# LayerNorm 1's weight and offset folded into the MoE modulation, its seeds moved to VectorE, and three pieces of work cut in halves

## What is computed

```python
u = x * (1 + sc1) + sh1                                    # modulation from the condition c
mix = concat(mLSTM heads(u), gated convolution(u)) @ w_out
x = layer_norm(ALPHA * x + (1 + gt1) * mix, ln1_g, ln1_b)  # LayerNorm 1
u = x * (1 + sc2) + sh2                                    # MoE modulation
y = hier_moe(u, ...)                                       # best of 4 groups, then 2 of its 4 experts
x = layer_norm(ALPHA * x + (1 + gt2) * y, ln2_g, ln2_b)    # LayerNorm 2
```

## Time and profile before

| | us |
|---|---|
| median of 3 runs | 835.89 (835.6 to 835.93) |
| profiled execution | 835.82 |
| its span in the trace | 834.1 |
| outside the span | 1.7 |
| PE busy | 795.4 (95% of the span) |
| DVE busy | 418.3 (50%) |
| HBM to chip, mean over the span | 359 GB/s |

### The profile page before, as it was taken

How to read it: one execution, slowest core, us unless ns; L and a number is a source line. 1 busy time by engine, 2 the same in 40 slices (tenths; PEclk the granted TensorE clock), 3 DMA queues, 4 the chain that set the end, 5 groups by cost and what they waited for, 6 DMA issues and landing times.

```text
span 834.1 us, 9198 instructions
## 1 busy us (share of the span) xinstructions
PE 795.4 (95%) x3779; PEld 419.0 (50%) x3801; DVE 418.3 (50%) x869; ACT 101.3 (12%) x237; POOL 29.1 (3%) x72
## 2 busy tenths in 40 slices
PE   8999999999999999999979999989899999999994
PEld 3575588445344434444347658844444434443431
DVE  0189888974423332332265985676533332333135
ACT  2111000023011001101111100002311101110110
POOL 3000000620000000000010000000000000000000
PEclk9999999999999999999999999999999999999998
DMA  9998998997999999999999699366699999999991
GB/s 317 389 387 315 388 388 328 362 380 297 390 412 414 415 411 413 415 411 412 411 388 337 224 359 386 140 248 255 226 383 411 414 415 409 415 416 409 414 391 57
DMA packets 90654, 299.29 MB, mean 359 GB/s; under 512 B 4153, under 2 KB 4441, under 8 KB 82417
## 3 DMA queue, kind: packets, MB, share of 16 engines
q1 hardware_dynamic: 86960, 291.60, 90.2%
q0 software_dynamic: 2592, 7.04, 2.2%
q10 hardware_dynamic: 1056, 0.03, 0.1%
HBM read 297.60 MB, written 1.05 MB: 358 GB/s over the span
## 4 chain that ended last, share of the span: by engine, by line
PE 85%; DMA 6%; DVE 4%; issue 3%; ACT 1%; POOL 1%; POOLq 0%; DVEq 0%; ACTq 0%
PE bank L647 22%; PE bank L603 17%; PE bank L671 12%; PE bank L634 8%; PE bank L620 7%; PE bank L828 7%; DMA ring<-in_w_up_dram 6%; PE bank L693 4%; PE bank L504 2%; PE bank L514 1%; PE bank L581 1%; PE bank L655 1%; PE bank L701 1%; ACT uT L923 1%; PE bank L531 0%
## 5 line engine op out<-in xcount | busy, mean ns | idle before, releaser
L603 PE MATMUL bank<-uT,ring 128*128 128x256 f32 x640 | 140.4, 380 | 0.0
L603 PEld LDWEIGHTS bank<-uT,ring 128*128 128x128 f32 x640 | 121.0, 190 | 19.6 <-issue 3.6
L647 PE MATMUL bank<-ring,qT 128*64 128x512 f32 x448 | 99.4, 594 | 2.8 <-issue 2.8
L671 PE MATMUL bank<-ring,hb 128*64 128x512 f32 x448 | 99.6, 595 | 1.4 <-ACT hb L949 1.4
L647 PE MATMUL bank<-ring,uT 128*64 128x512 f32 x448 | 99.2, 593 | 1.1 <-DMA ring<-in_w_up_dram 1.1
L1073 DVE SCALAR_TENSOR_TENSOR bench<-ring,cond,bench 128x512 f32<-128x512 f32 x126 | 94.7, 752 | 4.5
L1248 DVE SCALAR_TENSOR_TENSOR kT<-bank,share,gate_row 128x512 f32<-128x512 f32 x32 | 24.0, 749 | 90.0 <-PE bank L671 90.0
L634 PEld LDWEIGHTS bank<-ccT,X 128*128 128x128 f32 x512 | 61.5, 197 | 13.2 <-issue 11.4
L634 PE MATMUL bank<-ccT,X 128*128 128x128 f32 x512 | 64.6, 285 | 0.2
L647 PEld LDWEIGHTS bank<-ring,uT 128*64 128x64 f32 x448 | 31.6, 137 | 63.9 <-issue 60.2
L647 PEld LDWEIGHTS bank<-ring,qT 128*64 128x64 f32 x448 | 32.2, 137 | 61.7 <-issue 60.8
(11 more groups left out here) (252 smaller groups left out, 646.4 us busy)
## 6 DMA issues: line engine op xcount, KB each, us to landing
ring<-in_w_gate_dram SPq DMA_DIRECT2D x28, 2048.0 KB, 17.6
ring<-in_w_up_dram SPq DMA_DIRECT2D x28, 2048.0 KB, 17.8
ring<-in_w_down_dram SPq DMA_DIRECT2D x28, 2048.0 KB, 16.0
ring<-in_w_ada_dram SPq DMA_DIRECT2D x24, 2048.0 KB, 18.4
ring<-in_w_in_dram SPq DMA_DIRECT2D x14, 2048.0 KB, 17.7
ring<-in_w_out_dram SPq DMA_DIRECT2D x4, 2048.0 KB, 14.9
bench<-in_w_gate_dram SPq DMA_DIRECT2D x4, 2048.0 KB, 10.1
bench<-in_w_up_dram SPq DMA_DIRECT2D x4, 2048.0 KB, 17.8
```

The source lines that it names most:

```text
L603: last = pe.matmul(bank[4 + (b0 + q) % 4][:, 0:SEQ], w[:, kc, q * P:(q + 1) * P], uT[:, kc, :], start=(kc == 0), stop=(kc == KC - 1))
L647: last = pe.matmul(bank[bk][CAP * j:CAP * (j + 1), :], xg[b][:, 4 * h + k, CAP * j:CAP * (j + 1)], ring[s[h]][:, 4 * j + k, :], start=(h = ...
L671: last = pe.matmul(bank[6 + half][CAP * j:CAP * (j + 1), :], hhT[:, f, CAP * j:CAP * (j + 1)], ring[s[h]][:, 4 * j + 2 * i + half, :], sta ...
```

## The change

1. LayerNorm 1 leaves X without weight and offset: one `tensor_scalar` (subtract mean, times root) takes the place of `centre` and `finish`. `moe_shift_scale` takes weight and offset into scale and shift: scale' = scale * g, shift' = shift + scale * b. For that `b_ada_col` also holds columns of `ln1_g` and `ln1_b`, loaded at the start.
2. The seeds are ALPHA * (X * g + b). DVE writes them in pair 0, in eight instructions (`seed`); ACT's four copies go. POOL loads the rows of LayerNorm 2 only after `seeded`, because `seed` still reads those of LayerNorm 1.
3. The last block of the output projection (second token half, last 512 columns) is cut into two of 256 columns, the second in bank 7, and `add` follows piece by piece. `bn_stats` works on 256 columns everywhere.
4. X of the second token half is finished in column halves (`half_ready`, then `x_ready`), in both norms. The transposes follow half by half; for the MoE they run in the order `by_half` (chunks 0, 1, 4, 5, then 2, 3, 6, 7). One `stay_busy` matmul goes at the start of layer 1. The last output DMA becomes two.
5. `gate_up` waits for ACT's half of the gathered tokens before its first weight tile and for DVE's half before its second.
6. Of the small loads at the start, six become five, and these are bigger.

```diff
+        def out_pieces(t, half):
+            if t == 0 or half == 0:
+                return [(bank[2 * t + half][:, :], slice(0, COLS))]
+            return [(bank[3][:, 0:SEQ], slice(0, SEQ)), (bank[7][:, 0:SEQ], slice(SEQ, COLS))]
+
+        by_half = [c for half in range(2) for c in range(KC) if c // 2 % 2 == half]
+        in_halves = [(slice(0, COLS), half_ready), (slice(COLS, D), x_ready)]
...
+            sp.dma_start(b_moe_rows[4:6, :, :], ln1_g.rearrange("l (r n) -> r l n", n=COLS)).then_inc(cols_landed, 16)
+            sp.dma_start(b_moe_rows[6:8, :, :], ln1_b.rearrange("l (r n) -> r l n", n=COLS)).then_inc(cols_landed, 16)
...
+            for cols, done in in_halves:
+                sp.wait_ge(done, 2 * DEPTH if done is half_ready else 2 * T * DEPTH)
+                sp.dma_start(out[0, P:SEQ, cols], X[:, 1, cols]).then_inc(stored, 16)
...
                 load_gate_row(l, 1)
+                pool.wait_ge(seeded, l + 1)
                 load_norm_rows(l, 1)
...
-                pe.wait_ge(main.xg_act, n + 1)
-                pe.wait_ge(main.xg_dve, n + 1)
-                gate_up(4, b, s[0:2], lambda i: expert_arrived(pe, l, i, p), main.gate)
+                def here(i):
+                    pe.wait_ge((main.xg_act, main.xg_dve)[i], n + 1)
+                    expert_arrived(pe, l, i, p)
+
+                gate_up(4, b, s[0:2], here, main.gate)
...
-                    for t in range(T):
-                        transpose_half(t, x_ready, 2 * T * l - T + t + 1, straight)
-                        if t == 0:
-                            stay_busy(5, 5)
+                    transpose_half(0, [(x_ready, 2 * T * l - T + 1)] * 2, straight, range(KC))
+                    stay_busy(4, 5)
+                    transpose_half(1, [(half_ready, 2 * l), (x_ready, 2 * T * l)], straight, range(KC))
...
-                act.wait_ge(cleared, l + 1)
-                act.wait_ge(x_ready, 2 * T * l + T)
-                for b in range(4):
-                    last = act.activation(bank[b][:, :], X[:, b // 2, b % 2 * COLS:(b % 2 + 1) * COLS], ACT.Copy, scale=ALPHA)
-                last.then_inc(seeded, 1)
...
+                link(dve.tensor_tensor(view(scale2[:, :]), of[:, :, 2:4, :], view(scale), ALU.add))
+                dve.tensor_tensor(mod[:, 3, :], scale2[:, :], weight, ALU.mult)
+                dve.tensor_tensor(view(mod[:, 2, :]), of[:, :, 0:2, :], view(shift), ALU.add)
+                link(dve.tensor_tensor(offset2[:, :], scale2[:, :], offset, ALU.mult))
+                dve.tensor_tensor(mod[:, 2, :], mod[:, 2, :], offset2[:, :], ALU.add).then_inc(mod_moe_ready, 1)
...
                 def finish(t):
                     newton(t, 1, rs_ready, 2 * T * l + t + 1)
-                    dve.scalar_tensor_tensor(out=X[:, t, :], in0=X[:, t, :], scalar=rstd[:, t:t + 1],
-                                             in1=ln_b[:, :], op0=ALU.mult, op1=ALU.add).then_inc(x_ready, 1)
+                    for cols, done in ([(slice(0, D), x_ready)], in_halves)[t]:
+                        dve.tensor_scalar(X[:, t, cols], X[:, t, cols], mv[:, t, 0:1], rstd[:, t:t + 1],
+                                          ALU.subtract, ALU.mult).then_inc(done, 1)
...
+            def seed(l):
+                dve.wait_ge(rows_landed, 16 * (4 * l + 2))
+                dve.wait_ge(cleared, l + 1)
+                for b in range(4):
+                    cols = slice(b % 2 * COLS, (b % 2 + 1) * COLS)
+                    link(dve.scalar_tensor_tensor(out=tmp[:, :], in0=X[:, b // 2, cols], scalar=ALPHA, in1=ln_g[:, cols],
+                                                  op0=ALU.mult, op1=ALU.mult))
+                    last = dve.scalar_tensor_tensor(out=bank[b][:, :], in0=ln_b[:, cols], scalar=ALPHA, in1=tmp[:, :],
+                                                    op0=ALU.mult, op1=ALU.add)
...
                 for p in range(PAIRS):
                     n, b = PAIRS * l + p, p % 2
+                    if p == 0:
+                        seed(l)
                     if p + 1 < PAIRS:
                         xg_half(main, n + 1, 1 - b)
```

More of the change, by code:

```diff
@@ L328, in released @@
             elif kind == "wout":
[L329 removed]
+                eng.wait_ge(mix_done, 5 * l + (2, 5)[i])
             elif i >= 4:
@@ L575, in wait_block, with transpose_half @@
                         pe.wait_ge(proj_dve, 8 * l + b - 19)
-            def transpose_half(t, ready, value, cols):
-                pe.wait_ge(ready, value)
-                for kc in range(KC):
-                    last = pe.transpose(bank[2 * t + kc // 4][:, (kc % 4) * P:(kc % 4 + 1) * P], X[:, t, cols(kc)], ident[:, :])
-                    if kc % 4 == 3:
+            def transpose_half(t, ready, cols, order):
+                for i, kc in enumerate(order):
+                    if i % 4 == 0:
+                        pe.wait_ge(*ready[i // 4])
+                    last = pe.transpose(bank[2 * t + i // 4][:, (i % 4) * P:(i % 4 + 1) * P], X[:, t, cols(kc)], ident[:, :])
+                    if i % 4 == 3:
                         last.then_inc(xT_ready, 1)
@@ L826, in _ @@
                     for t in range(T):
-                        for kc in range(KC):
-                            last = pe.matmul(bank[2 * t + half][:, :], mixT[:, kc, t * P:(t + 1) * P], w[:, kc, :],
-                                             start=(kc == 0), stop=(kc == KC - 1))
-                        last.then_inc(mix_done, 1)
+                        for to, cols in out_pieces(t, half):
+                            for kc in range(KC):
+                                last = pe.matmul(to, mixT[:, kc, t * P:(t + 1) * P], w[:, kc, cols],
+                                                 start=(kc == 0), stop=(kc == KC - 1))
+                            last.then_inc(mix_done, 1)
                 pe.wait_ge(weighed, turn(l, 9))
                 four_sums(6, l, (4, 5, 8, 9), moe_sum)
-                transpose_half(0, x_ready, 2 * T * l + 1, rows_of)
+                transpose_half(0, [(x_ready, 2 * T * l + 1)] * 2, rows_of, by_half)
                 pe.wait_ge(moe_copied, l + 1)
@@ L1152, in moe_shift_scale @@
                 of = bank[6][:, :].rearrange("p (m j g r) -> p m g j r", m=2, j=2, g=4)[:, :, :, :, 0]
-                shift_scale(l, 1, of[:, :, 0:2, :], of[:, :, 2:4, :], lambda c: c.rearrange("p (m h j) -> p m h j", m=2, h=2),
-                            mod_moe_ready)
+                view = lambda c: c.rearrange("p (m h j) -> p m h j", m=2, h=2)
+                shift, scale, weight, offset = [b_ada_col[:, l, (3 + v) * KC:(4 + v) * KC] for v in range(4)]
+                link(dve.tensor_tensor(view(scale2[:, :]), of[:, :, 2:4, :], view(scale), ALU.add))
@@ L1160, in add @@
-                    cols = slice(half * COLS, (half + 1) * COLS)
-                    link(dve.tensor_tensor(tmp[:, :], bank[2 * t + half][:, :], gate_row[:, cols], ALU.mult))
-                    link(dve.scalar_tensor_tensor(out=X[:, t, cols], in0=X[:, t, cols], scalar=ALPHA,
-                                                  in1=tmp[:, :], op0=ALU.mult, op1=ALU.add))
-                    link(dve.bn_stats(stats[:, t, half, :], X[:, t, cols]))
+                    for piece, (mix, cols) in enumerate(out_pieces(t, half)):
+                        ours = slice(half * COLS + cols.start, half * COLS + cols.stop)
+                        dve.wait_ge(mix_done, 5 * l + 2 * half + t + piece + 1)
+                        link(dve.tensor_tensor(tmp[:, cols], mix, gate_row[:, ours], ALU.mult))
+                        link(dve.scalar_tensor_tensor(out=X[:, t, ours], in0=X[:, t, ours], scalar=ALPHA,
+                                                      in1=tmp[:, cols], op0=ALU.mult, op1=ALU.add))
+                        for q in range(ours.start // SEQ, ours.stop // SEQ):
+                            last = dve.bn_stats(stats[:, t, q, :], X[:, t, q * SEQ:(q + 1) * SEQ])
```

70 lines of the change are left out of this document (35 added, 35 removed).

## The result

| | before | after |
|---|---|---|
| median of the first comparison, us | 835.75 (835.6 to 835.93, 4 runs) | 828.18 (827.27 to 830.12, 4 runs) |
| profiled execution / its span | 835.82 / 834.1 | 828.24 / 826.4 |
| all executions, later ones included | 833.9 (830.56 to 836.42, 70 runs) | 828.9 (827.27 to 830.29, 16 runs) |

The ratio of the first comparison is 0.9913, with an interval of 0.9895 to 0.993. Over all executions it is 0.9941 (0.9930 to 0.9951, medians resampled): 4.9 us faster. One more execution of the kernel before, of 1405.94 at a mean granted clock of 0.55, is left out throughout. The forecast was 833.3, with a range from 831.0: the kernel gained more than that by either measure. The first four runs of the kernel before agreed within 0.33 us, and yet lay 1.9 us above what the same kernel takes on the whole.

The account below looks back on a forecast made before the run. The weight stream, restarted by PE's start of pair 0, bounds each MoE. Each layer -2.15 + 1.1 = -1.05, twice -2.1; then -0.4 - 0.2 + 0.2: -2.5 from 835.82 gives 833.3 us, range 831.0 to 836.4.

Parts of the forecast that it names:

- the reference: Starting time of the sum: the profiled execution, 835.82 us, within 0.1 of the median of three runs, so no correction.
- Passage up to the routing: Passage to the MoE, edits 1, 3, 4: PE's second routing matmuls start earlier, -0.8 us in each layer (-0.4 to -0.9).
- rival (d): Passage to the MoE: folded modulation later than thought, ACT ends no earlier, nothing gained up to the routing; 834.9 us, chance 0.08.
- First gather: Pair 0 of the MoE, edit 5: PE starts without waiting for DVE's half, -1.35 us in each layer.
- Seeds: DVE in pair 0, edit 2: eight instructions, 6.3 us, fit into DVE's idle 8.36 us; cost 0.
- Rows: LayerNorm 2's row loads, edit 2: now behind the weight stream's restart, +1.1 us in each layer (1.0 to 2.54).
- (a): Rival on LayerNorm 2's row loads: paid in full, 2.54 us in each layer; 836.2 us, no change; chance 0.20.
- (b): Rival on LayerNorm 2's row loads: not felt, or by 0.15 us only; 831.4 us, chance 0.15.
- (c): Rival on the weight stream: row loads and weights together lower its rate, costing 3.7 us; 838.5 us, chance 0.07.
- Start of layer 1: Layer 1's first transposes: one `stay_busy` matmul less and X's first half earlier, -0.4 us once (0 if X is late).
- End: Last output DMA carries half as much, the last pass's halves take 0.1 more: -0.2 us once (0 to -0.5).
- Start: Small loads at the kernel's start have a few more bytes ahead of tiles PE awaits: +0.2 us once (0 to 0.4).

## Why the prediction was wrong

The mechanisms held, but sizes and the reference did not. The measured 828.18 lies 5.1 below the forecast. Some 2.0 of that are mis-sized terms of the sum, 2.6 the reference, and 0.4 are left. Step by step, at equal clock:

- **Passage up to the routing**: forecast -0.8, measured -1.11. ACT was named as becoming as late as VectorE; it is the later one. The mis-sized step is ACT's, not the five small instructions: the folded modulation is there 3.36 after VectorE's start, as worked out, but ACT starts 3.39 after it and not 3.51, its twelve chunks take 4.31 and not 4.4, and PE follows after 0.05 and not 0.14. ACT ends at 183.95 and VectorE at 183.80. That the pieces gain nothing here was right, and rival (d), a passage that gains nothing, falls.
- **First gather**: forecast -1.35, measured -1.45. The forecast let the gate start when the transpose of `pmax` ends; measured, the gate starts 0.20 after that transpose does and 0.07 ahead of its end. Twice that is -2.9 of the -4.5 below.
- **Seeds**: forecast 0, right. They take 5.8 us, where 6.3 were expected, and end 1.18 ahead of the tokens of pair 1.
- **Rows**: forecast +1.1, measured +1.0 against the same kernel with the loads gone or early, and 2.56 for the second pair. The bounds (1.0 to 2.54) stand. So does the reason, for the larger part: poor stretches are filled, (381 - 321) x 4 / 413 + (418 - 367) x 5 / 413 = 1.2 of 2.54. That would leave 1.3; a part of it lies under PE's own time, which the forecast did not reckon with, since without rows PE is the bound. Against the kernel before, the stage is only 0.67 longer, because that kernel waits for tiles too, by 0 to 1 us from one trace and layer to the next. The sum had no term for this: I took the stage of the kernel before as fixed, from one trace. Twice 0.43 of the miss lie here. Rivals (a), (b) and (c) all fall: paid in full, not felt, and a lower rate.
- **Start of layer 1**: forecast -0.4. With the clock at 0.86, as in the kernel before, it is -0.23 (14.57 with two pairs of rows, 14.58 without any, 14.80 before). In the kernel after itself the clock is at 0.72 to 0.78 there, and it is +0.66. The step "With one less, and with the first half of X there 0.6 earlier, they start 0.4 earlier" took the clock of one trace for the clock of the changed kernel. The low clock is not edit 4's: with edit 5 alone the stage is 15.40, and the kernel after gains nothing against that (15.39 to 15.50), nor do the halves (15.47 without). What sets the clock there is open. The lower clock is dearer here and comes with a full clock in layer 1's projection, where two of three traces of the kernel before lose 1.7. The four zeros matmuls of the kernel after take nearly what five took before:

```profile
426.18 1.91 PE L521 MATMUL bank<-zeros 128*128 128x512 bf16 x4
```

- **End**: forecast -0.2, measured -0.53. From the end of VectorE's last pass to the end of the span it takes 2.8 instead of 3.45: the halved output DMA is worth 0.6, where the forecast had 0.3, less 0.1 for the pass.
- **Start**: forecast +0.2, measured 0 (31.99 with edit 6 alone and 32.03 without, at the same clock).

Sum: 2 x (-1.11 - 1.45 + 0.67) - 0.23 - 0.53 = -4.5, where -2.5 was forecast. With the table's sixth and seventh rows (+0.66 and -1.1) in place of the -0.23 it is -4.8; the runs as a whole say -4.9. The 2.6 us by which the first comparison lies beside the whole of the runs come on top; 0.4 of its 7.6 are then left, of the size of what the clock does to a median. The step that failed there is the reference: I wrote "That execution stands within 0.1 of the median of the three runs", and made no correction. Three runs in one place do not say how a kernel scatters; seventy say 830.6 to 836.4. With 833.9 as the reference and my sum the forecast would have been 831.4, still 2.4 above the 828.9 that came.

## What to carry to other kernels

A wait for two halves of an operand, made by two engines, is worth splitting where the consumer works half by half: one wait gave two thirds of this gain by the stages, and 3.8 of 4.9 us by the medians. Bytes that the stream has to carry were free ahead of its standstill (217.5 with them and without them) and cost 1.0 in each layer behind the restart, so look for a buffer that is idle there before you let a load wait for the one in use. And before a forecast of half a per cent, look for stretches of low granted clock in the trace: what lies there can be that execution's alone, and a change may not find it there again.

## What the runs showed of the hardware

- TensorE's clock goes to its half at a few places of an otherwise busy kernel, and whether it does differs between executions of the same program: the six zeros matmuls shown lose 1.15 to one such place, layer 1's projection loses 1.7, and the mean granted clock goes with the times, which scatter over 5.9 us. The Trainium skill, "TensorE: Matmul & The Clock Gate", "What's actually happening", calls the number of slow matmuls at a start variable from run to run and puts the penalty of that ramp below 1% of a typical kernel's span. No run here measures the ramp alone, and here low stretches come in the middle of a kernel too; the scatter of all runs of the kernel before is 0.7%. That is more than most single edits here are worth.
- A low clock at the start of layer 1 (0.72 to 0.78) came always with a full clock in the projection after it, in eight traces; with 0.86 there the projection was slow in three of six. I have no explanation.
- `tensor_scalar` over 1024 fp32 columns in SBUF takes 0.81 (0.50 for 512), `scalar_tensor_tensor` 1.28. The Trainium skill, "VectorE: DVE Perf Modes", "Mode 2×_2P — use both read ports for one tensor", has fp32 at double rate for the first and not where a second tensor is read, which `scalar_tensor_tensor` does here; the trace agrees in direction, with a ratio of 1.6 for the whole instruction.
